# Key numbers by exclusive-or and minimum, a norm's end in two fused operations, and eight value rows moved behind the norms

## The reference, cut to what matters

```python
def layer_norm(x, g, b):
    mu = jnp.mean(xf, axis=-1, keepdims=True)
    var = jnp.mean(jnp.square(xf - mu), axis=-1, keepdims=True)
    y = (xf - mu) * lax.rsqrt(var + LN_EPS)
    return y.astype(x.dtype) * g + b
...
    s_half, i_half = lax.top_k(s, PEER_TOPK)              # 16 best of 128 keys, two halves, 8 heads
    cand = s_half[:, :, 0, :, None] + s_half[:, :, 1, None, :]
    cand_idx = i_half[:, :, 0, :, None] * N_KEYS + i_half[:, :, 1, None, :]
    top_s, top_pos = lax.top_k(cand.reshape(...), PEER_TOPK)   # 16 best of 256 sums
    experts = jnp.take_along_axis(cand_idx.reshape(...), top_pos, axis=-1)
    gates = jax.nn.softmax(top_s, axis=-1)
...
        a = jax.nn.gelu(jnp.einsum('tkd,td->tk', expert_u[es], xs), approximate=False)
        return jnp.einsum('tk,tkd->td', gs * a, expert_v[es])
```

## Time and profile before

| | |
|---|---|
| three runs | 1995.32, 1997.62, 1999.78 us |
| profiled execution | 2003.31 us, its span 2001.5 us |
| TensorE busy | 1843.9 us, 92% of the span |
| VectorE busy | 1322.7 us, 66% |
| GpSimd busy | 902.6 us, 45% |
| granted TensorE clock, mean | 0.968 |
| HBM traffic | 333 GB/s over the span |

### The profile page before, as it was taken

How to read it: one execution, slowest core, us unless ns; L and a number is a source line. 1 busy time by engine, 2 the same in 40 slices (tenths; PEclk the granted TensorE clock), 3 DMA queues, 4 the chain that set the end, 5 groups by cost and what they waited for, 6 DMA issues and landing times.

```text
span 2001.5 us, 21759 instructions
## 1 busy us (share of the span) xinstructions
PE 1843.9 (92%) x8148; PEld 1192.6 (60%) x8148; DVE 1322.7 (66%) x2597; ACT 285.1 (14%) x660; POOL 902.6 (45%) x837
## 2 busy tenths in 40 slices
PE   5888999989999889998999999997789989999994
PEld 1675744457544337997888888885444434434441
DVE  1111585689668778999998876669856523326767
ACT  0120110046300001111110010006530000000000
POOL 1010137567535422325355555557756565435440
PEclk9999999989999989999999999999989999999997
DMA  8895849898899977539999999998889989999994
GB/s 351 349 363 208 342 147 334 288 332 307 294 371 335 341 306 283 201 131 360 351 362 351 394 369 408 409 402 310 295 300 410 409 346 409 409 409 405 409 410 184
DMA packets 166714, 670.24 MB, mean 335 GB/s; under 512 B 19370, under 2 KB 19498, under 8 KB 160972
## 3 DMA queue, kind: packets, MB, share of 16 engines
q0 software_dynamic: 112512, 410.79, 54.9%
q1 hardware_dynamic: 49344, 242.24, 30.6%
q10 hardware_dynamic: 4752, 15.81, 2.1%
HBM read 659.27 MB, written 7.39 MB: 333 GB/s over the span
## 4 chain that ended last, share of the span: by engine, by line
PE 55%; DMA 22%; DVE 11%; POOL 8%; issue 4%; ACT 1%; ACTq 0%; DVEq 0%; POOLq 0%
PE psum L785 22%; DMA arena<-in_expert_v_dram,arena 11%; POOL arena L513 7%; PE psum L932 7%; DMA arena<-in_expert_u_dram,arena 6%; PE psum L848 5%; PE psum L862 3%; PE psum L865 3%; DVE arena L1343 2%; PE psum L897 2%; PE psum L813 2%; DMA arena<-in_w_ada_dram 2%; PE psum L874 1%; PE psum L872 1%; PE psum L648 1%
## 5 line engine op out<-in xcount | busy, mean ns | idle before, releaser
L513 POOL DMA_INDIRECT arena<-in_expert_u_dram,arena x384 | 479.6, 1249 | 370.6 <-DVE arena L1343 236.7
L1343 DVE CUSTOM_DVE_ANT_0 arena<-arena 128x1024 f32<-128x1024 f32 x384 | 462.2, 1227 | 198.7 <-DMA arena<-in_expert_u_dram,arena 197.8
L513 POOL DMA_INDIRECT arena<-in_expert_v_dram,arena x384 | 378.9, 987 | 411.8 <-DVE psum L1574 207.3
L1574 DVE SCALAR_TENSOR_TENSOR psum<-arena,psum 128x1024 f32<-128x1024 f32 x254 | 327.1, 1288 | 213.3 <-DMA arena<-in_expert_v_dram,arena 202.5
L785 PE MATMUL psum<-arena 128*128 128x256 f32 x2048 | 445.2, 381 | 5.3 <-DMA arena<-in_expert_uT_dram 5.3
L848 PE MATMUL psum<-arena 128*128 128x512 f32 x1024 | 444.5, 596 | 0.1
L785 PEld LDWEIGHTS psum<-arena 128*128 128x128 f32 x2048 | 391.3, 191 | 58.0 <-issue 5.7
L848 PEld LDWEIGHTS psum<-arena 128*128 128x128 f32 x1024 | 194.7, 191 | 252.4 <-issue 252.4
L932 PE MATMUL psum<-arena 128*128 128x128 f32 x1280 | 146.3, 276 | 0.4 <-DVE arena L1488 0.4
L932 PEld LDWEIGHTS psum<-arena 128*128 128x128 f32 x1280 | 144.5, 192 | 1.5 <-issue 0.9
L660 PE MATMUL psum<-arena 128*128 128x512 f32 x320 | 137.7, 593 | 0.0
(11 more groups left out here) (174 smaller groups left out, 1452.9 us busy)
## 6 DMA issues: line engine op xcount, KB each, us to landing
arena<-in_expert_uT_dram SPq DMA_DIRECT2D x128, 512.0 KB, 6.8
arena<-in_expert_v_dram SPq DMA_DIRECT2D x128, 512.0 KB, 6.8
arena<-in_w_in_dram SPq DMA_DIRECT2D x16, 2048.0 KB, 10.6
arena<-in_w_ada_dram SPq DMA_DIRECT2D x12, 2048.0 KB, 14.2
arena<-in_w_query_dram SPq DMA_DIRECT2D x8, 2048.0 KB, 13.7
arena<-in_w_in_dram SPq DMA_DIRECT2D x16, 512.0 KB, 8.1
arena<-in_w_o_dram SPq DMA_DIRECT2D x4, 2048.0 KB, 13.4
arena<-in_expert_u_dram,arena POOLq DMA_INDIRECT x384, 8.9
```

What stands on the lines that cost most here:

```text
L513: pool.indirect_dma_start(slots[b], None, table[0], bass.IndirectOffsetOnAxis(ap=numbers[:, b - b0:b - b0 + 1], axis=0)).then_inc(lands[b] ...
L1343: dve.tensor_tensor_reduce(UR[b], UR[b], U2B[e], 1.0, 0.0, ALU.mult, ALU.add, DOTS[e % 2][:, k:k + 1]).then_inc(u_free, 1)
L1574: dve.scalar_tensor_tensor(ys, row, weight, ys, ALU.mult, ALU.add).then_inc(v_free, 1)
```

## The change

Three edits. First, the key numbers: each of the 16 best keys of a half gets its number with its rank in the bits above it (number or rank*256, made once a tile with an or in place of the cast; `RANKS` holds rank*256 and is set once). The wanted digits are shifted up by eight bits too. Then an exclusive-or of wanted digit and numbered key is the bare key number where the rank is the wanted one and at least 256 elsewhere, so that a minimum over the 16 gives it: two passes of 2048 elements in place of three. Second, a norm ends in (x - mean) * gain, ahead of the wait for the square root, and (that) * rstd + shift. Third, of the eleven value rows behind the last merge step eight go into the steps of tile 1's selection. The counts of the semaphores follow (LNS 12 to 11, FIN 10 to 9, ROUTE_AT).

```diff
             def normed(step, base, out, gain, shift, sqrt_sem, sqrt_count):
 
+                dve.scalar_tensor_tensor(out, out, MV[:, 0:1], gain, ALU.subtract, ALU.mult).then_inc(step, 1)
                 dve.wait_ge(sqrt_sem, sqrt_count)
                 dve.reciprocal(RSTD[:, 1:2], RSTD[:, 0:1]).then_inc(step, 1)
-                dve.wait_ge(step, base + 5)
-                dve.tensor_scalar(out, out, MV[:, 0:1], RSTD[:, 1:2], ALU.subtract, ALU.mult).then_inc(step, 1)
                 dve.wait_ge(step, base + 6)
-                dve.tensor_tensor(out, out, gain, ALU.mult).then_inc(step, 1)
-                dve.wait_ge(step, base + 7)
-                dve.tensor_tensor(out, out, shift, ALU.add).then_inc(step, 1)
+                dve.scalar_tensor_tensor(out, out, RSTD[:, 1:2], shift, ALU.mult, ALU.add).then_inc(step, 1)
...
             dve.wait_ge(consts_in, 48)
+            dve.tensor_scalar(RANKS, IOTA[:, 0:TOPK], float(NEXT), None, ALU.mult).then_inc(ranks_set, 1)
             convolve(0)
...
                 def key_numbers(side):
 
                     digit = digits[side].rearrange("p (h k) -> p h k", k=TOPK)
-                    done(dve.tensor_tensor(eq, digit.unsqueeze(3).to_broadcast(cube), iota, ALU.is_equal))
+                    wanted = (PA, POS)[side].rearrange("p (h k) -> p h k", k=TOPK)
+                    done(dve.tensor_tensor(found, wanted.unsqueeze(3).to_broadcast(cube),
+                                           numbered[:, :, side, :].unsqueeze(2).to_broadcast(cube), ALU.bitwise_xor))
                     settle()
-                    done(dve.tensor_tensor(eq, eq, idxf[:, :, side, :].unsqueeze(2).to_broadcast(cube), ALU.mult))
-                    settle()
-                    done(dve.tensor_reduce(digit, eq, AX, ALU.add))
+                    done(dve.tensor_reduce(digit, found, AX, ALU.min))
...
-                    done(dve.tensor_copy(IDXF, IDXS))
+                    done(dve.tensor_tensor(NUMBERED.rearrange("p (m k) -> p m k", k=TOPK),
+                                           IDXS.rearrange("p (m k) -> p m k", k=TOPK),
+                                           RANKS.unsqueeze(1).to_broadcast([P, 2 * PEER_HEADS, TOPK]), ALU.bitwise_or))
...
-                    done(dve.tensor_scalar(PA, POS, 4, None, ALU.logical_shift_right))
+                    done(dve.tensor_scalar(PA, POS, 4, 8, ALU.logical_shift_right, ALU.logical_shift_left))
                     done(dve.tensor_copy(place, POS))
-                    done(dve.tensor_scalar(POS, POS, TOPK - 1, None, ALU.bitwise_and))
+                    done(dve.tensor_scalar(POS, POS, TOPK - 1, 8, ALU.bitwise_and, ALU.logical_shift_left))
                     settle()
                     done(dve.tensor_copy(digits[0], PA))
                     done(dve.tensor_copy(digits[1], POS))
+                    done(dve.tensor_scalar(place, place, float(NEXT), None, ALU.mult))
                     settle()
-                    done(dve.scalar_tensor_tensor(digits[0], place, float(8 + 8 - KEPT), digits[0], ALU.add, ALU.max))
-                    done(dve.scalar_tensor_tensor(digits[1], place, float(KEPT - 8), digits[1], ALU.is_lt, ALU.mult))
+                    done(dve.scalar_tensor_tensor(PA, place, float(NEXT * (8 + 8 - KEPT)), digits[0], ALU.add, ALU.max))
+                    done(dve.scalar_tensor_tensor(POS, place, float(NEXT * (KEPT - 8)), digits[1], ALU.is_lt, ALU.mult))
...
-MERGE_ROWS, NORM_ROWS = 11, 2
-CHOICE_ROWS = (7, 3, 3, 3, 3, 3, 2, 2, 2, 4, 0)
+MERGE_ROWS, NORM_ROWS = (11, 11, 11, 11, 11, 11, 11, 3), 2
+CHOICE_ROWS = (9, 4, 4, 4, 4, 3, 3, 3, 3, 3, 0)
```

More of the change, by code:

```diff
@@ L43 @@
 KEPT = CAND // 2
+NEXT = 256
 GROUP = 8
@@ L249, in backbone @@
         SMAX, TOPS, GSUM = keep(HK), keep(PEER_HEADS, TOPK), keep(PEER_HEADS)
+        RANKS = keep(TOPK).bitcast(U32)
+        NUMBERED = IDXF.bitcast(U32)
         POS, PA, AF, BF = SW[:, 0, :].bitcast(U32), SW[:, 1, :].bitcast(U32), SW[:, 2, :], SW[:, 3, :]
@@ L321, in backbone @@
         gated, placed = sem("gated"), sem("placed")
-        product = sem("product")
+        product, ranks_set = sem("product"), sem("ranks_set")
         zero_set, rank_done, rank_out = sem("zero_set"), sem("rank_done"), sem("rank_out")
@@ L1364, in route @@
                 val = VAL.rearrange("p (h s k) -> p h s k", s=2, k=TOPK)
-                idxf = IDXF.rearrange("p (h s k) -> p h s k", s=2, k=TOPK)
+                numbered = NUMBERED.rearrange("p (h s k) -> p h s k", s=2, k=TOPK)
                 cube = [P, PEER_HEADS, TOPK, TOPK]
                 if part == 0:
+                    dve.wait_ge(ranks_set, 1)
                     dve.wait_ge(topk_step, 80 * (TURN[e] + 1))
@@ L1389, in route @@
                 cands = CANDS[e][:, :, 0:KEPT].rearrange("p h (a b) -> p h a b", b=TOPK)
[L1390 removed]
+                found = EQ[e].bitcast(U32).rearrange("p h (a b) -> p h a b", b=TOPK)
                 pos = POS.rearrange("p (h k) -> p h k", k=TOPK)
                 smax = SMAX.rearrange("p (h k) -> p h k", k=TOPK)
[L1393 removed]
                 digits = DIGITS[e] if e in DENSE else (AF, BF)
@@ L1478, in section @@
                     if s == 1:
-                        values(MERGE_ROWS * i, MERGE_ROWS * (i + 1))
+                        values(sum(MERGE_ROWS[:i]), sum(MERGE_ROWS[:i + 1]))
                 for e in tiles:
@@ L1493, in section @@
                     normed(ln_step, base + 2, xr, PRM[s][1], PRM[s][2], sqrt_done, e + 1)
+                    dve.wait_ge(ln_step, base + 9)
+                    dve.tensor_tensor(u2, xr, PRM[s][3], ALU.mult).then_inc(ln_step, 1)
                     dve.wait_ge(ln_step, base + 10)
-                    dve.tensor_tensor(u2, xr, PRM[s][3], ALU.mult).then_inc(ln_step, 1)
-                    dve.wait_ge(ln_step, base + 11)
                     dve.tensor_tensor(u2, u2, PRM[s][4], ALU.add).then_inc(ln_step, 1)
                     if s == 1:
-                        values(8 * MERGE_ROWS + NORM_ROWS * (e - 1), 8 * MERGE_ROWS + NORM_ROWS * e)
+                        values(sum(MERGE_ROWS) + NORM_ROWS * (e - 1), sum(MERGE_ROWS) + NORM_ROWS * e)
                 if s == 0:
@@ L1686, in _ @@
                 finish(e)
-LNS = 12
-FIN = 10
+LNS = 11
+FIN = 9
 SUB_AT = 3 + 5 * PEER_HEADS + 1
-ROUTE_AT = (0, 3 + PEER_HEADS, 3 + 3 * PEER_HEADS, SUB_AT, SUB_AT + 10, SUB_AT + 13, SUB_AT + 17)
+ROUTE_AT = (0, 3 + PEER_HEADS, 3 + 3 * PEER_HEADS, SUB_AT, SUB_AT + 10, SUB_AT + 12, SUB_AT + 16)
 PARTS = len(ROUTE_AT) - 1
@@ L1710 @@
 assert (HK - BESIDE) % (2 * GROUP) == 0 and BESIDE % (2 * GROUP) == 0 and GATE_ROUNDS % 4 == 0
-MERGE_ROWS, NORM_ROWS = 11, 2
-CHOICE_ROWS = (7, 3, 3, 3, 3, 3, 2, 2, 2, 4, 0)
-assert 8 * MERGE_ROWS + 4 * NORM_ROWS + sum(CHOICE_ROWS) == HK and len(CHOICE_ROWS) == 5 + PARTS
+MERGE_ROWS, NORM_ROWS = (11, 11, 11, 11, 11, 11, 11, 3), 2
+CHOICE_ROWS = (9, 4, 4, 4, 4, 3, 3, 3, 3, 3, 0)
+assert sum(MERGE_ROWS) + 4 * NORM_ROWS + sum(CHOICE_ROWS) == HK and len(CHOICE_ROWS) == 5 + PARTS
 CTX_ROWS = (32, 56)
```

## The result

The changed kernel takes 1981.62 us, median of four runs (1980.36 to 1983.80), beside 1998.43 us for the kernel before in the same measurement (1995.32 to 1999.78): a ratio of 0.9905, 95% interval 0.9887 to 0.9923. The forecast was 1980.0 us in a range of 1975 to 1988. The medians lie 16.8 us apart, where the sum said 17.6. The profiled execution took 1982.75 us, its span 1980.9, mean granted TensorE clock 0.972.

What follows compares the result with a forecast made beforehand. TensorE, busy 92% of the span, was taken to bound most of it, with turns among engines and full DMA engines later. Gains of 14.0 us at the gates and 3.6 in the tail gave 1980.0 us, range 1975.0 to 1988.0.

Steps and rivals of the forecast that it cites:

- The front: Tile 0's selection up to the window pass: the shorter selection shifts the whole rest 4.0 us earlier, bounds 0 and 4.5.
- The eight rows and the norms in the merge: Last merge step to second query block: moved rows and shorter norms start that block 11.0 us earlier.
- TensorE from there to the gates: Second query block to placing: TensorE runs with one gap of 5.3 us, at its first expert block, keeping 15.0 us.
- VectorE's path: Merge through tile 1's and three more selections to the gates: 7.5 us earlier at tile 1's rows, 14.4 at the gates.
- freed issues: Selections before the gates: without the removed two-input pass, gathers issue earlier, giving half of the shortened gap back.
- The smaller gain decides: At the gates, where VectorE's one-hot passes and TensorE's placing meet: 15.0 against about 14.4 us, taken as 14.0.
- The norms: End of each norm: 1.2 us saved; three successive norms in the tail give 3.6 us.
- The sum: Whole kernel: 14.0 us at the gates plus 3.6 in the tail, 17.6 us saved.
- A changed length of this stretch: Sign of a wrong forecast: the stretch behind the gates, expected to keep its length, changes it.
- TensorE alone decides, or more: Rival at the gates: refills keep up, clock and gathers gain from shorter stalls; 18.6 to 22 us, at 1977.5; chance 0.20.
- The slow integer passes: Rival in the selections: integer passes run at a lower rate; at 4.6 us each, 21 us slower, 2019; chance 0.05.
- Gathers decide: Rival at the gates: shortened gaps return as waits, VectorE gains 7.5 to 11 us, kernel 1985.0 us; chance 0.22.

Runs made afterwards that it cites:

- e3: Only the key numbers changed, against the kernel before: 1993.56 us, ratio 0.9969 (0.9955 to 0.9984).
- e7: The changed kernel plus six redundant two-input passes in the selections of tiles 3, 4 and 2: 2010.99 us, ratio to the kernel before 0.9926 (0.9903 to 0.9949).
- e8: The changed kernel plus six redundant minima in the selections of tiles 3, 4 and 2: 2007.92 us, ratio to the kernel before 0.9895 (0.9868 to 0.9922).
- e1: Only the eight value rows moved, against the kernel before: 2000.61 us beside 1998.25, ratio 1.0002 (0.9986 to 1.0017).
- e4: Rows and norms changed, key numbers as in the kernel before: 1997.03 us, ratio 0.9983 (0.9966 to 1.0000).

## Why the prediction was right

**The front** (4.0): 3.97 in the profiled pair, and for the reason given: TensorE's own scores cap what the window pass can gain. In nine of the ten traces with the new passes VectorE waits there for TensorE (1.6 to 3.3 us); in e3 it does not, and the matmul gains 0.55. Single executions scatter: the marked matmul starts between 417.74 and 419.71 in the four kernels with the old passes, and between 412.54 and 417.77 with the new ones.

**The eight rows and the norms in the merge** (11.0): 11.1 to 11.5 against the last merge matmuls. TensorE's whole gain at the second query block was 14.55 for 15.0. The rows alone are worth 9.6 there. The output projection still waits for its weights (5.73 us for 5.36), so part of the front is lost there: the last merge matmuls come 3.46 us earlier, the projection 3.10.

**TensorE from there to the gates**: the text took the one gap as unchanged. It grew from 5.30 to 6.26 us, and 13.34 us arrive. This is the largest miss of a size on the deciding path, but the gap takes 2.94 to 6.98 us over all traces, so it is scatter as far as the runs show.

**VectorE's path** (7.5 at tile 1's first row, 14.4 at the gates): 6.4 and 15.44. The middle between all and nothing was a choice, not worked out, and it was about right, which is partly luck: the stretch became 9.0 us shorter in the pair, and over all kernels 456.7 us on average with the old passes became 450.4 with the new (6.3 of 13.8; the text had 6.9). The reason given for it, freed issues, is not shown: issues do stretch beside two-input passes, but e7 and e8, which were to price that, differ by less than the scatter.

**The smaller gain decides** (14.0): 13.3. That the later path decides holds: e1 and e4 show TensorE waiting for VectorE, e3 VectorE for TensorE. Which one it is came out the other way: the text had VectorE's 14.4 below TensorE's 15.0, and in the trace TensorE's 13.34 is below VectorE's 15.44. TensorE gained less and VectorE more than stated, and that the smaller of the two still came near 14.0 is luck. With the average 6.3 us in place of the 9.0 of this execution, VectorE's gain would be 12.7, so in other executions it may be the later one.

**The norms** (1.2 each): 1.22, and the tail 3.7 for 3.6; the fused passes are 0.05 us dearer than taken, which the shorter gaps make up.

**The sum**: 13.3 + 3.7 = 17.0 against 16.8 by the medians. The profiled pair differs by 20.6, and 3.6 of that lie between placing and the last rows (622.3 us before, 618.7 after). A changed length of this stretch was one of the text's signs of being wrong. But in e1 to e4, with the same code there, it takes 616.3 to 620.5, so the profiled execution of before was a long one; the text had said so of its 5.7 us above the median.

**The rivals.** That TensorE's path decides whatever VectorE does falls by e1. The text's "TensorE alone decides, or more" is half right: TensorE did come last in the changed kernel, but with 13.3 us and not the 15.0 to 18.4 of that rival, and the refills did not keep up wholly (15.44 us of 21.2). The slow integer passes fall by the 2.29 us. "Gathers decide" gave VectorE 7.5 to 11 us; it gained 15.44, 2.1 more than TensorE, in this execution.

## What to carry to other kernels

Where two engines meet, find both paths' slack there before pricing a change: rows alone and norms alone were worth 0 and 0.3%, key numbers alone 0.3%, together 0.95%. Price a moved piece by what it waits for at its old and its new place, and then by what is next in line there: eight rows of 1.29 us (10.3) held VectorE for 20.6 us and were worth 9.6 to TensorE, and seven more of them, moved to the wrong side of a block of weight loads, made the merge 22 us later. Work removed between refills comes back in part as waits: of 13.8 us removed, 9.0 were kept in the profiled pair and 6.3 on average over the traces, and of 13.7 us added 2 to 5 showed.

## What the runs showed of the hardware

Integer passes of VectorE (exclusive-or and minimum over uint32, the minimum into float32) take 2.29 us for 128x2048 elements, like float ones. A gather's issue of 0.94 us stretched to 2.02 and 3.05 us beside a two-input pass of 2.29 us, with the exception in e8, and not beside a reduction. With the DMA engines full (417 GB/s from 690 to 720 us in the changed kernel) and 2 MB weight loads among the transfers, one gather (128 rows, 512 KB) lands every 6.17 us. The same kernel took 27 to 30 us more in later measurements on two other chips (2025.7 and 2028.7 for 1998.4), with the loss in places that the code does not name: stops of TensorE of 0.2 to 1.7 us, and 21.4 us behind a load's issue for which the profile shows no cause.
